# Moving tiles and outputs of the three-product matmuls, walked in 16-column pieces from the last to the first, the two halves in turn

## The reference

```python
def swiglu(x, w_gate, w_up, w_down):
    return (jax.nn.silu(x @ w_gate) * (x @ w_up)) @ w_down
...
        x = x + 0.5 * swiglu(rms_norm(x, ffn1_norm[l]), ffn1_w_gate[l], ffn1_w_up[l], ffn1_w_down[l])
        h = rms_norm(x, mix_norm[l])
        proj = h @ w_in[l]
...
        x = x + jnp.concatenate([o_a, o_b], axis=-1) @ w_out[l]
        x = x + 0.5 * swiglu(rms_norm(x, ffn2_norm[l]), ffn2_w_gate[l], ffn2_w_up[l], ffn2_w_down[l])
```

## Time and profile before

| what | value |
|---|---|
| median of three runs | 2691.41 us (2689.9, 2691.41, 2701.05) |
| profiled execution: span from first to last instruction | 2690.7 us |
| mean granted clock of TensorE | 0.988 |
| PE busy, weight loads busy | 97%, 86% of the span |
| DVE busy, ACT busy | 63%, 40% |
| DMA | 380.98 MB, mean 142 GB/s |
| three-product matmuls of the six lines, counted in the built program | 5,850 with 512 columns, 8,052 with 256 |
| of the 8,052: in line with the weights | 1,116 |

### The profile page before, as it was taken

The page is one execution under the profiler, slowest core; times in us unless marked ns, Lnnn a source line. Parts: engine busy times, 40 slices in busy tenths (PEclk is TensorE's granted clock), DMA queues, the critical chain, the costliest instruction groups (busy, mean ns, idle before and its releaser), DMA issues.

```text
span 2690.7 us, 38911 instructions
## 1 busy us (share of the span) xinstructions
PE 2603.1 (97%) x15924; PEld 2305.4 (86%) x15924; DVE 1693.8 (63%) x2685; ACT 1083.8 (40%) x1686; POOL 64.2 (2%) x60
## 2 busy tenths in 40 slices
PE   7999899999999999999999999999999999998998
PEld 7998789899888888778888888889888888888998
DVE  6767555777777655656644777755555446786664
ACT  5546643555322224344253422223322234555553
POOL 0001021000000000000000000000000000000000
PEclk9999899999999999999999999999999999999999
DMA  7764201576455443111223455543444433244454
GB/s 262 235 230 175 86 9 48 191 236 208 150 178 189 169 150 103 50 47 63 94 91 98 135 190 178 180 162 111 141 133 137 133 113 111 78 131 157 169 193 147
DMA packets 110113, 380.98 MB, mean 142 GB/s; under 512 B 12016, under 2 KB 17392, under 8 KB 109552
## 3 DMA queue, kind: packets, MB, share of 16 engines
q1 hardware_dynamic: 108928, 373.32, 42.2%
q10 hardware_dynamic: 1008, 5.18, 0.5%
HBM read 377.40 MB, written 1.05 MB: 141 GB/s over the span
## 4 chain that ended last, share of the span: by engine, by line
PE 88%; DVE 5%; ACT 4%; issue 2%; DMA 0%; SPq 0%; ACTq 0%; DVEq 0%
PE B L1458 25%; PE B L1460 25%; PE B L1459 25%; ACT w_hi L1779 2%; DVE w_lo L2075 2%; PE B L1718 1%; PE B L1701 1%; PE B L1473 1%; PE B L1611 1%; PE B L1474 1%; PE B L1625 1%; PE B L1475 1%; PE B L1618 1%; PE B L1708 1%; DVE AC L2324 1%
## 5 line engine op out<-in xcount | busy, mean ns | idle before, releaser
L1458 PE MATMUL B<-U,w_hi 128*128 128x256 f32 (+1 forms) x2896 | 962.1, 332 | 6.3 <-DVE w_lo L2075 6.2
L1459 PE MATMUL B<-U,w_hi 128*128 128x256 f32 (+1 forms) x2896 | 952.8, 329 | 0.0
L1460 PE MATMUL B<-U,w_lo 128*128 128x256 f32 (+1 forms) x2896 | 952.6, 329 | 0.0
L2075 DVE TENSOR_TENSOR w_lo<-w_raw,w_hi 128x1024 fp32r<-128x1024 f32 (+3 forms) x587 | 685.5, 1180 | 410.1 <-ACT w_hi L1779 409.0
L1779 ACT ACTIVATE w_hi<-w_raw 128x1024 fp32r<-128x1024 f32 (+3 forms) x587 | 591.0, 1012 | 500.1 <-PE B L1460 477.8
L1458 PEld LDWEIGHTS B<-U,w_hi 128*128 128x128 f32 x2896 | 547.1, 189 | 62.9 <-issue 8.2
L1459 PEld LDWEIGHTS B<-U,w_hi 128*128 128x128 f32 x2896 | 546.7, 189 | 53.3 <-issue 2.2
L1460 PEld LDWEIGHTS B<-U,w_lo 128*128 128x128 f32 x2896 | 546.7, 189 | 51.4
L1458 PE MATMUL B<-HHf,w_hi 128*128 128x256 f32 (+1 forms) x1122 | 364.3, 325 | 1.8 <-DVE w_lo L2075 1.8
L1460 PE MATMUL B<-HHf,w_lo 128*128 128x256 f32 (+1 forms) x1122 | 363.5, 324 | 0.0
L1459 PE MATMUL B<-HLf,w_hi 128*128 128x256 f32 (+1 forms) x1122 | 363.5, 324 | 0.0
(11 more groups left out here) (352 smaller groups left out, 2620.2 us busy)
## 6 DMA issues: line engine op xcount, KB each, us to landing
w_raw<-in_w SPq DMA_DIRECT2D x504, 512.0 KB, 4.3
w_ada<-in_w SPq DMA_DIRECT2D x144, 512.0 KB, 3.4
w_raw<-in_w SPq DMA_DIRECT2D x58, 384.0 KB, 3.1
w_raw<-in_w SPq DMA_DIRECT2D x16, 240.0 KB, 2.5
X<-in_x SPq DMA_DIRECT2D x2, 1024.0 KB, 9.6
w_raw<-in_w SPq DMA_DIRECT2D x8, 256.0 KB, 2.6
BW<-in_bias ACTq DMA_DIRECT2D x1, 1536.0 KB, 10.3
K<-in_consts ACTq DMA_DIRECT2D x2, 640.0 KB, 4.9
```

The costliest lines, as they stand in the source:

```text
L1458: pe.matmul(o, hi, xh, start=i == 0 and s.start, stop=False)
L1459: pe.matmul(o, hi, xl, start=False, stop=False)
L1460: e = pe.matmul(o, lo, xh, start=False, stop=i == last and s.stop)
L2075: dve.tensor_tensor(w_lo[:, plan.slot[u], 0:n], w_raw[:, plan.ring[u], 0:n], w_hi[:, plan.slot[u], 0:n].bitcast(F32), ALU.subtract).then_i ...
```

## The change

A helper `inward` gives another view of the same columns, and the moving tile and the output of each three-product matmul are taken through it:

```diff
+    def inward(ap):
+
+        return ap.rearrange("p (h a b) -> p a h b", h=2, b=16)[:, ::-1]
+
     def tensor(pe):
...
             if k == "gemm":
-                o, c, last = PS(s.b, s.o + s.n, s.m)[:, s.o:s.o + s.n], slice(s.o, s.o + s.n), len(s.wts) - 1
+                o, c, last = inward(PS(s.b, s.o + s.n, s.m)[:, s.o:s.o + s.n]), slice(s.o, s.o + s.n), len(s.wts) - 1
                 for i, wt in enumerate(s.wts):
                     hi, lo = weight(wt)
-                    xh, xl = HI[s.x][:, s.k0 + i, c], LO[s.x][:, s.k0 + i, c]
+                    xh, xl = inward(HI[s.x][:, s.k0 + i, c]), inward(LO[s.x][:, s.k0 + i, c])
...
-                    o, k = PS((s.b, s.b2)[i % 2])[:, c], s.k0 + i // 2
+                    o, k = inward(PS((s.b, s.b2)[i % 2])[:, c]), s.k0 + i // 2
                     hi, lo = weight(wt)
+                    xh, xl = inward(HI[s.x][:, k, c]), inward(LO[s.x][:, k, c])
...
-                    pe.matmul(o, hi, HI[s.x][:, k, c], start=k == 0, stop=False)
-                    pe.matmul(o, hi, LO[s.x][:, k, c], start=False, stop=False)
-                    e = pe.matmul(o, lo, HI[s.x][:, k, c], start=False, stop=k == 7)
+                    pe.matmul(o, hi, xh, start=k == 0, stop=False)
+                    pe.matmul(o, hi, xl, start=False, stop=False)
+                    e = pe.matmul(o, lo, xh, start=False, stop=k == 7)
```

## The result

The change made the kernel slower: 2742.57 us median of four runs (2739.65 to 2745.03) against 2690.65 (2688.2 to 2701.05) before, ratio 1.019 with a 95% interval of 1.017 to 1.021. The forecast was 2634, and the time lies just above the end of the range, 2735.

A forecast was written before the change was run, and what follows sets the result against it. The prediction took the pace at which three-product matmuls follow one another on PE as the bound. Gains of 50 us (512 columns) and 7 us (256 in line), the rest 0, summed to -57 us: 2634 us, range 2605 to 2735.

The forecast's parts named there:

- Term 1: 5,850 matmuls of 512 columns in line: start distance from 226.5 to 218 ns, a gain of 50 us.
- Term 2: 1,116 matmuls of 256 columns in line with the weights: distance from 120.6 to 114.5 ns, a gain of 7 us.
- Term 3: 6,936 matmuls of 256 columns 48 floats off: no change taken; gain at most 14 us, loss up to 49 us.
- Term 4: Later waits as faster PE asks for weights sooner: taken as 0, up to 5 us given back in the mixers.
- The upper bounds: Worst distances allowed: 512 columns 233 ns, loss 38 us; 256 in line, loss 8; 256 off line 120.6, loss 49.
- The order does not matter: Rival: no effect on matmul distances, 2691 us (2685 to 2700), including a mixed case of gains and losses; chance 0.20.
- Each jump costs: Rival: slower, a new jump after every 16 columns in moving tile and output, 32 per 512-column matmul; chance 0.13.
- The two walks run together and collide: Rival: slower, moving-tile and weight reads collide, with losses in one placement and gains in the other; chance 0.10.

The follow-up runs named there:

- m4_lines: Measuring kernel, groups of 48 matmuls alone, walking 4 (8, 2) columns of each 64 bytes or larger steps; 223.4 ns for 4 columns in line, straight 226.7.
- k_output: The changed kernel with only the outputs walked inward, moving tiles straight; 2693.65 us, ratio 0.998 to the kernel before.
- m1_walks: Measuring kernel, groups of 48 matmuls alone, varying walk, piece size, placement and walked operand; 512 columns in line: inward 233.3 ns, output alone inward 226.7 once settled.
- k_onward: The changed kernel with the same pieces, halves in turn, walked from first to last instead of reversed; 2799.17 us, ratio 1.036 to the kernel before.
- m2_places: Measuring kernel, groups of 48 matmuls alone, shifting moving tile and weights, weights of 2 to 128 columns; straight 512 columns 231.7 ns with weights of 2.
- k_lines_inline: The kernel before, with tiles in line and those of 512 columns walked 4 columns of each 64 bytes, four passes; 2691.94 us, ratio 0.998.
- k_lines: The kernel before, with only 512-column moving tiles and outputs walked 4 columns of each 64 bytes, four passes; 2695.65 us, ratio 1.000.

## Why the prediction was wrong

**What bounds the kernel: right.** Waits, counts and transfers stayed, the distances alone moved, and their sum gives the 51 us.

**Term 1, 512 columns in line, 226.5 to 218 (-50 us): wrong in sign.** They went to 233.3 and 230.0, and 512 columns together cost +30 us. The failing step is the reading that "the reads of the moving tile and those of the next matmul's weights meet", and that this meeting is what a walk can win back. With weights of 2 columns the straight walk still has 231.7, 16 ns over the 215.8 of the same 4 columns, so most of what is lost lies within the read of the moving tile, and there was no meeting of that size to be avoided. The 218 was an estimate that no run shows: the fastest full walk of 512 columns found beside weights of 128 has 223.4 (m4_lines), inward by itself 226.7 to 233.4. The lower bound of 216.7 is the time of an fp32 record, and no fp32r matmul of 512 columns with a full walk came to it. In which order the weights are read, on which the gain rested, and whether "the two walks" meet at all, no run shows. What a wide load in line does add is of the other sign: it takes straight 512 columns down (231.7 to 226.7) and inward not (230.0 to 230.0 or 233.4). I had the hint in hand and explained it away: the matmuls of 256 columns with weights of 16 still stood at 115 (1.61 us for 14), which I took as saying that little was left to gain for 256 columns, when it said that the weights weren't the cause.

**Term 2, 256 in line, 120.6 to 114.5 (-7 us): wrong,** 119.9 to 120.7, a loss of about 1 us. Here the reading had something to it: with weights of 2 columns straight 256 columns have 113.5, so the load in line does cost them 6 ns. But walking inward doesn't win that back.

**Term 3, 256 columns 48 floats off, unchanged (0): +24 us with what else 256 columns did.** They went to 117.3, about half way to the upper bound of 120.6, which I had kept for the range.

**Term 4, later waits (0): right,** -3 us.

**The upper bounds were better than the value taken.** The worst placement seen, 233, was what 512 columns came to, by luck: it was the distance of a straight tile in another placement, and inward had 236.5 in one group. The row to be nearest to was not the fp32 one, where 216.7 ns goes to 256 columns and not to 512, but the fp32r ones.

**The rivals.** "The order does not matter" fell: 226.7, 233.3 and 240.0 stand for three orders of one tile. The straight walk by itself has 226.7 to 233.3, by placement. "Each jump costs" fell as a mechanism: the output has the same jumps for nothing (k_output), the time doesn't follow the number of jumps (m1_walks), and the same 4 columns 128 times over are at 215.8. Its full price, 13.3 and 6.7 ns a matmul or 132 us, which the range leaves out, no run shows as a price of jumps: an output in pieces of 16 columns cost nothing (0.998 for the kernel), and the dearest walk, onward, cost 99 us (2799 against 2700.5). "The two walks run together and collide" came nearest in its signs: losses where tiles of 512 columns are in line, and a placement against the weights at which the loss is gone (226.7 at 48 floats in the groups by themselves; in the kernel 227.0 and 236.5 stand side by side). Its full price was 512 columns at 233 and those of 256 off the line at 120.6, +38 and +49 us, 2778; no run shows the second, which came to 117.3. A collision may be what takes inward from 230.0, its distance without weights to meet, to 233.4; that is argued and not shown, and it is the smaller part of what lies over 215.8.

**PE's two reads.** That the reads of moving tile and weights disturb each other is shown as far as the difference of placement changes the distance with weights of 128 columns (226.7 to 233.3 straight) and does not with 2 (231.7 at the two placements tried). The bulk, the 16 ns of straight over 215.8 with weights of 2 columns, isn't explained by it.

**Chances.** 0.24 for slower was too little for a change whose gain rested on an inference that no row showed (the direction in which weights are read), while its likely losses stood in rows.

## What to carry to other kernels

Read PE's rate from the distances between starts, by form and by stage, and expect it to depend on how the moving tile lies and is walked: in fp32r the versions of this kernel had stages at 223 to 240 ns for 512 columns, a spread of 7%, and k_onward lost 3.6% of the whole by it. Keep the moving tile one straight run unless a measurement says otherwise; beside a straight moving tile, an output walked in pieces of 16 columns (inward, onward or back) cost nothing at 512 columns in line (226.7 each once settled, as straight). When a row with one suspect nearly removed (weights of 16 columns) still shows the loss, that suspect is not the cause, and groups of 48 matmuls by themselves settle such a question in one run; but a gain of 1 to 2% found that way has to be confirmed in the kernel, where the same walk may settle at another distance.

## What the runs showed of the hardware

- The same 4 moving columns over and over: 215.8 ns for 512. The same 16: 243.3. Straight: 226.7 to 233.3, by the placement against weights of 128 columns modulo 256 bytes (m2_places), and 231.7 with weights of 2. Halves in turn, forward: 240.0, 0.469 ns a column, with weights of 2 as with 128, and with weights of 2 at all lengths from 128 to 512.
- Four columns of each 64 bytes, in four passes: 223.4 in line and 231.8 at 48 floats off, the first of them the fastest full walk found beside weights of 128 columns. With 2 columns at a time, in tile and output, 431 to 447; with steps of 128 and 256 bytes 240 to 249 and 276 to 279.
- One stream of identical matmuls has several steady distances: 226.7 or 236.7, 230.0 or 233.3, 226.7 or 223.3, and for 256 columns 113.3, 114.3 or 117.8. Most stages keep the one they have for up to hundreds of us; it can change where the moving tile does, without a wait (114.5 to 117.8 at 139.1 us of k_lines_inline). The flip in k_lines alone was worth 7 us, 0.3% of the kernel, so differences of that size say little unless the distances are read stage by stage.
- What resource is behind it stays open: no run separates the order of 16-byte groups from the order of 64-byte places in a way that explains both lines() at 223 and its larger steps at 277. What makes one stream settle at one distance or another is open too.
